# Three slots in lockstep at the RMS joints, constants multiplied while waiting, and a changed head and tail

## The reference

```python
def first_block(x, ...):
    for layer in range(2):
        x = x + 0.5 * rmsnorm(swiglu(rmsnorm(x, g[0]), gate0, up0, down0), g[1])
        x = x + rmsnorm(token_mixer(rmsnorm(x, g[2]), ...), g[3])
        x = x + 0.5 * rmsnorm(swiglu(rmsnorm(x, g[4]), gate1, up1, down1), g[5])

def second_block(x, ...):
    for l in range(2):
        proj = x @ w_in[l]
        mix = concatenate([hgrn2_mixer(...), nsa_mixer(...)]) @ w_out[l]
        x = layer_norm(ALPHA * x + mix, ...)
        x = layer_norm(ALPHA * x + swiglu(x, gate, up, down), ...)
```

## Time and profile before

| | us |
|---|---|
| median of 3 runs | 3538.73 (3535.65 to 3539.88) |
| the profiled execution, its own time | 3540.74 |
| its span, first to last instruction | 3538.9 |
| PE busy in it | 3402.1 (96%) |
| DVE, ACT, POOL busy | 1611.7, 1260.4, 1354.5 |

### The profile page before, as it was taken

How to read it: one execution, slowest core, us unless ns; L and a number is a source line. 1 busy time by engine, 2 the same in 40 slices (tenths; PEclk the granted TensorE clock), 3 DMA queues, 4 the chain that set the end, 5 groups by cost and what they waited for, 6 DMA issues and landing times. The chain is left out here.

```text
span 3538.9 us, 47749 instructions
## 1 busy us (share of the span) xinstructions
PE 3402.1 (96%) x17526; PEld 2702.6 (76%) x17526; DVE 1611.7 (46%) x2820; ACT 1260.4 (36%) x2129; POOL 1354.5 (38%) x582
## 2 busy tenths in 40 slices
PE   8999999999999999999999999989999999889998
PEld 6888866688878888766788878767888787568886
DVE  4441445554335432363644255774331358753322
ACT  3222346522232222265422244463222343642222
POOL 3444222244434444322344433304444443134443
PEclk9999999999999999999999999999999999999999
DMA  4222311222222222211222332202222321112222
GB/s 174 95 99 95 115 66 43 66 95 95 95 83 97 99 97 95 107 60 36 84 95 94 98 130 69 71 19 71 96 95 96 113 92 51 47 54 96 100 95 84
DMA packets 86780, 306.19 MB, mean 87 GB/s; under 512 B 11205, under 2 KB 11717, under 8 KB 85358
## 3 DMA queue, kind: packets, MB, share of 16 engines
q1 hardware_dynamic: 86400, 304.18, 25.6%
q10 hardware_dynamic: 238, 0.09, 0.0%
HBM read 299.49 MB, written 4.74 MB: 86 GB/s over the span
## 5 line engine op out<-in xcount | busy, mean ns | idle before, releaser
L338 POOL TENSOR_TENSOR wL<-ring,wH 128x1024 fp32r<-128x1024 f32 x513 | 1258.1, 2452 | 2112.3 <-ACT wH L328 2048.4
L288 PE MATMUL bank<-hH,wH 128*128 128x512 f32 x2448 | 966.0, 395 | 11.0 <-DVE yT L989 4.8
L328 ACT ACTIVATE wH<-ring 128x1024 fp32r<-128x1024 f32 x522 | 548.3, 1050 | 1157.5 <-PE bank L290 972.9
L290 PE MATMUL bank<-hH,wL 128*128 128x512 f32 x2448 | 954.5, 390 | 0.0
L289 PE MATMUL bank<-hL,wH 128*128 128x512 f32 x2448 | 953.7, 390 | 0.0
L288 PEld LDWEIGHTS bank<-hH,wH 128*128 128x128 f32 x2448 | 460.6, 188 | 111.6 <-issue 6.3
L290 PEld LDWEIGHTS bank<-hH,wL 128*128 128x128 f32 x2448 | 460.1, 188 | 96.9
L289 PEld LDWEIGHTS bank<-hL,wH 128*128 128x128 f32 x2448 | 460.6, 188 | 95.3 <-issue 1.9
L288 PE MATMUL bank<-guH,wH 128*128 128x512 f32 (+1 forms) x1292 | 502.9, 389 | 2.3 <-ACT early L1385 1.4
L290 PE MATMUL bank<-guH,wL 128*128 128x512 f32 (+1 forms) x1292 | 496.2, 384 | 0.0
L289 PE MATMUL bank<-guL,wH 128*128 128x512 f32 (+1 forms) x1100 | 418.6, 381 | 0.0
(11 more groups left out here) (347 smaller groups left out, 3863.9 us busy)
## 6 DMA issues: line engine op xcount, KB each, us to landing
ring<-in_w SPq DMA_DIRECT2D x376, 512.0 KB, 3.5
ring<-in_down SPq DMA_DIRECT2D x96, 448.0 KB, 3.2
ring<-in_down SPq DMA_DIRECT2D x48, 512.0 KB, 3.5
ring<-in_next SPq DMA_DIRECT2D x12, 512.0 KB, 3.4
mix<-in_table SPq DMA_DIRECT2D x2, 2560.0 KB
mix<-spread SPq DMA_DIRECT2D x4, 768.0 KB, 6.1
mix<-row SPq DMA_DIRECT2D x1, 2560.0 KB
spread<-mix SPq DMA_DIRECT2D x1, 2560.0 KB, 8.0
```

The source lines that it names most:

```text
L288: eng.matmul(out, a, hi, start=first, stop=False)
L290: return eng.matmul(out, b, hi, start=False, stop=last)
L328: eng.activation(parts_of(n, per)[0][:, 0:width], ring[:, n % NSLOT, 0:width], ACT.Copy).then_inc(w_hi, 1)
L338: eng.tensor_tensor(l[:, 0:width], ring[:, n % NSLOT, 0:width], h[:, 0:width], ALU.subtract).then_inc(w_lo, 1)
```

## The change

- The head makes three slots instead of two: slot 0 follows the pieces of hH and hL, slots 1 and 2 take their high part first and their low part last. ACT's gain load goes behind the three loads for the bias table; the squares go behind the third high part; DVE makes the low part of slot 1, POOL those of slots 2 and 3; SP loads five slots. The bias row is spread by one DMA from HBM to HBM.
- The four joints multiply three slots in lockstep (`joint_of`), the fourth slot's high part is made between chunks (`act_split`) and its low part by DVE after the last chunk. The third slot's high part stands ahead of the root, its low part ahead of DVE's first scaled chunk. Three more slots use dead tiles (`placed`).
- `keep_warm` multiplies the identity by constants into an unused PSUM bank: in `pe_stat_out` before and after the second statistics matmul. No result of it is read.
- Before the second FFN the squares go to PSUM banks 3 and 7, DVE adds them in another order, and ACT takes the high parts after columns 1, 3, 5 and 7.
- In block two, projection slot 2 is multiplied ahead of the layer's block, after the pair; five slots are loaded ahead instead of four.
- In the tail the mean is copied to SBUF, and POOL subtracts it from columns 4 to 7.

The diff, cut to what the prediction speaks of:

```diff
-        def pe_stat_out(eng, r):
+        def pe_stat_out(eng, r, before, after, into):
 
             eng.wait_ge(sq_used, 8 * r + 7 + 2)
             eng.matmul(bank[6][:, :], onesD, acc, start=True, stop=False, skip_group_check=True)
+            keep_warm(eng, before, into, S // 2)
             eng.wait_ge(sq_ready, 8 * r + 8)
             eng.matmul(bank[6][:, :], onesD, sq[:, 1, :], start=False, stop=True,
                        skip_group_check=True).then_inc(stat_ready, 1)
+            keep_warm(eng, after, into)
...
+        def act_split(eng, xr, gains, fourth):
...
+                if m == 4:
+                    hi(eng, fourth)
+                eng.wait_ge(x_ready, xr + m + 1)
+                eng.activation(hH[:, m, :], xT[:, m, :], ACT.Copy, scale=gains[:, m:m + 1]).then_inc(h_hi, 1)
+                eng.activation(yT[:, m, :], xT[:, m, :], ACT.Square).then_inc(xsq_ready, 1)
...
         def dve_post(eng, q, n, g, third, h0=None, gains=None, b=None):
...
+            vector_lo(eng, third)
             eng.wait_ge(rs_ready, q + 1)
-            vector_lo(eng, third)
+            vector_lo(eng, third + 1)
...
+        JOINT_BANKS = (0, 2, 1)
+
+        def joint_of(eng, n, h0, banks):
+
+            landed(eng, n + len(banks) - 1)
+            for kc in range(KD):
+                eng.wait_ge(h_hi, h0 + kc + 1)
+                for u, b in enumerate(banks):
+                    high, low = (v[:, kc * P:(kc + 1) * P] for v in parts_of(n + u))
+                    eng.matmul(bank[b][:, :], high, hH[:, kc, :], start=(kc == 0), stop=False, skip_group_check=True)
+                    eng.matmul(bank[b][:, :], low, hH[:, kc, :], start=False, stop=False, skip_group_check=True)
+                eng.wait_ge(h_ready, h0 + kc + 1)
+                for u, b in enumerate(banks):
+                    mm = eng.matmul(bank[b][:, :], parts_of(n + u)[0][:, kc * P:(kc + 1) * P], hL[:, kc, :],
+                                    start=False, stop=(kc == KD - 1), skip_group_check=True)
+                    if kc == KD - 1:
+                        mm.then_inc(slots_done, 1)
+
+        def keep_warm(eng, times, into, columns=S):
+
+            for _ in range(times):
+                eng.matmul(bank[into][:, 0:columns], ident, mats[:, 0:columns // P, :], start=True, stop=True,
+                           skip_group_check=True)
...
-            if n0:
-                eng.wait_ge(g_free, KF * c + 1)
+            eng.wait_ge(g_free, KF * c + 2)
+            if norm is not None:
                 pair_of(eng, n0, h0)
-            eng.wait_ge(g_free, KF * c + 2)
-            slot(0, 1, 0)
+                slot(0, 1, 0)
+            elif n0:
+                joint_of(eng, n0, h0, JOINT_BANKS)
             slot(0, 1, 1)
...
-                dve_y(eng, r, KD - 1)
+                eng.wait_ge(sq_ready, 8 * r + 8)
+                eng.tensor_copy(yT[:, KD - 1, :], bank[5][:, :]).then_inc(y_done, 1)
+                eng.wait_ge(stat_ready, 2 * r + 2)
+                eng.sem_inc(sq_used, 1)
...
-            if n0 and not third:
-                hi(eng, n0 + 2)
-            hi(eng, n0 + 3)
+            if stat is None:
+                hi(eng, n0 + 3)
...
             if not halves:
+                hi(eng, n0 + FFN_SLOTS + 2)
                 act_root(eng, q + 1, EPS_RMS)
...
+        OUT_SQ = (3, 7)
+
         def act_out1(eng):
 
             for m in range(KD):
                 eng.wait_ge(y_done, 8 + m + 3)
                 eng.wait_ge(sq_used, 8 + m + 1)
-                eng.activation(sq[:, m % 2, :], yT[:, m, :], ACT.Square).then_inc(sq_ready, 1)
-                if m in (1, 4, 6):
-                    hi(eng, n_out + A1 + 2 + (1, 4, 6).index(m))
+                to = bank[OUT_SQ[m % 2]][:, :] if m < KD - 1 else sq[:, 1, :]
+                eng.activation(to, yT[:, m, :], ACT.Square).then_inc(sq_ready, 1)
+                if m in (1, 3, 5, 7):
+                    hi(eng, n_out + A1 + 2 + (1, 3, 5, 7).index(m))
 
         def dve_out1(eng):
+
+            def add(m):
+                eng.wait_ge(sq_ready, 8 + m + 1)
+                if m == 0:
+                    eng.tensor_copy(acc, bank[OUT_SQ[0]][:, :]).then_inc(sq_used, 1)
+                    return
+                eng.wait_ge(sq_used, 8 + m + 2)
+                eng.tensor_tensor(acc, bank[OUT_SQ[m % 2]][:, :], acc, ALU.add).then_inc(sq_used, 1)
 
             eng.wait_ge(early_out, KD)
             for m in range(KD):
+                if m:
+                    add(m - 1)
                 eng.wait_ge(*tile_end(n_out + A1, B1, m, KD - 1))
                 eng.tensor_tensor(yT[:, m, :], bank[4 + m % 2][:, :], early[:, m, :], ALU.add).then_inc(y_done, 1)
-                if m:
-                    add_squares(eng, 1, m - 1)
-            add_squares(eng, 1, KD - 1)
+            eng.wait_ge(stat_ready, 4)
+            eng.sem_inc(sq_used, 1)
...
+            def high(n, kc, v, first=False):
+                return eng.matmul(bank[JOINT_BANKS[n]][:, :], parts_of(n)[0][:, kc * P:(kc + 1) * P], v[:, kc, :],
+                                  start=first, stop=False, skip_group_check=True)
+
+            def low(n, kc):
+                return eng.matmul(bank[JOINT_BANKS[n]][:, :], parts_of(n)[1][:, kc * P:(kc + 1) * P], hH[:, kc, :],
+                                  start=False, stop=(kc == KD - 1), skip_group_check=True)
+
+            eng.wait_ge(w_hi, 1)
+            for kc in range(KD + 1):
+                if kc < KD:
+                    eng.wait_ge(h_hi, kc + 1)
+                    high(0, kc, hH, kc == 0)
+                if kc:
+                    if kc == 1:
+                        landed(eng, 0)
+                    eng.wait_ge(h_ready, kc)
+                    high(0, kc - 1, hL)
+                    mm = low(0, kc - 1)
+            mm.then_inc(slots_done, 1)
+            for n in (1, 2):
+                eng.wait_ge(w_hi, n + 1)
+                for kc in range(KD):
+                    high(n, kc, hH, kc == 0)
+                    high(n, kc, hL)
                 landed(eng, n)
                 for kc in range(KD):
+                    mm = low(n, kc)
...
                 sp.dma_start(t["row"], rows8).then_inc(w_in1, 16)
-                for n in range(2, 4):
+                sp.dma_start(mats[:, :, :], t["mats"]).then_inc(par_in, 16)
+                for n in range(2, 5):
                     load(sp, n, t["first"][n, :, :], WIDE)
-                sp.dma_start(mats[:, :, :], t["mats"]).then_inc(par_in, 16)
                 sp.wait_ge(w_in1, 16)
 
-                sp.dma_start(spread, t["row"].unsqueeze(0).broadcast_to([P, NSA, 640])).then_inc(w_in1, 16)
-                sp.wait_ge(w_in1, 32)
-                sp.dma_start(t["spread"], spread).then_inc(bias_out, 16)
-                slot_sem(sp, 3)
+                sp.dma_start(t["spread"], t["row"].unsqueeze(0).broadcast_to([P, NSA, 640])).then_inc(bias_out, 16)
+                slot_sem(sp, 4)
...
-                act.dma_start(gnext, t["gfirst"]).then_inc(x_in[0], 16)
                 act.dma_start(onehot, t["onehot"]).then_inc(tab_in, 16)
                 act.dma_start(rb[0:32, :], t["rel_bias"]).then_inc(tab_in, 16)
                 act.dma_start(rb[32:33, :], t["one8"]).then_inc(tab_in, 16)
+                act.dma_start(gnext, t["gfirst"]).then_inc(x_in[0], 16)
                 act.preload_act_table_set(EXP_LN)
                 hi(act, 0)
-                act_split(act, None, gnext, True, early_slot=1)
+                for m in range(KD):
+                    if m == 2:
+                        hi(act, 1)
+                    act.wait_ge(x_in[m // 2], 16 if m // 2 else 32)
+                    act.activation(hH[:, m, :], xT[:, m, :], ACT.Copy, scale=gnext[:, m:m + 1]).then_inc(h_hi, 1)
                 hi(act, 2)
+                for m in range(KD):
+                    act.activation(yT[:, m, :], xT[:, m, :], ACT.Square).then_inc(xsq_ready, 1)
+                hi(act, 3)
 
             @block.vector
             def _(dve):
                 for n, c in enumerate((0, 320)):
                     dve.wait_ge(c_out, n + 1)
                     dve.tensor_copy(rows8[:, c:c + 320], bank[4 + n][0:8, 0:320]).then_inc(c_done, 1)
-                vector_lo(dve, 0)
+                dve.wait_ge(w_hi, 1)
+                dve.tensor_tensor(parts_of(0)[1], ring[:, 0, :], parts_of(0)[0], ALU.subtract).then_inc(w_lo, 1)
                 for m in range(KD):
                     rest(dve, 0, m, gnext)
+                vector_lo(dve, 1)
...
             def _(pool):
-                los(pool, 1, 3)
+                los(pool, 2, 4)
...
+                       n_ffn1: (place(guH, 16), place(guH, 18), n_out + A1),
+                       n_next: (place(guH, 0), place(guH, 2), n_next - 2),
+                       n_next + 2: (place(guH, 4), place(guH, 6), n_next - 2)})
...
-                    stream(sp, layer, t["next_1"], 0, 4, n_next, WIDE)
-                    slot_sem(sp, n_next + 3)
```

(50 more changed lines are left out.)

76 lines of the change are left out of this document (25 added, 51 removed).

## The result

The changed kernel takes 3522.3 us (median; 3518.2 to 3525.2 in 4 runs) against 3537.9 for the kernel before on the same chip: a ratio of 0.9949, 95% interval 0.9937 to 0.9961. The forecast was 3522.6. The profiled span is 3523.2 us against 3538.9.

What follows compares the result with a forecast made beforehand. PE, busy 96% of the span, was taken as the bound; only its idle, half clock, head and tail could save time. 7.6 + 10.2 + 2.3 - 1.6 - 4.6 + 2.2 = 16.1 off 3538.73 gave 3522.6 us, range 3512 to 3533.

Steps and rivals of the forecast that it cites:

- Head: Start of the kernel to the first layer block: slot 3 starts at 30.5 instead of 39.21; 7.6 us gained (4 to 10).
- rival D: Head: loads and tables queue behind the HBM to HBM bias spread, slower from 32 us of transfer on; chance 0.05.
- Joints before the FFN: Two RMS joints before block one's second FFNs: slot 3 begins at 690.2 instead of 695.26; 5.1 us each, 10.2 in both.
- Ln comes about 1.5 earlier: Joints before the FFN: with squares in PSUM, DVE's adds take 0.7, so Ln comes 1.5 us earlier (0.5 to 1.8).
- priced half clock at half its length: RMS joints: half-clock stretches of 6.9 us before and 3.4 us behind the FFN cost half their length and go.
- Joint after the FFN: Block one, layer 0: slot 3 starts at 1063.1 instead of 1066.55, less 1.1 for the sums; 2.3 us gained (1 to 5).
- Into block two: Joint into the second block: a new 3.2 us wait ahead of slot 6, plus half clock; -1.6 us (-4 to +3.2).
- Layer 0 to 1: Second block, between its layers: the block opens 5.5 us later; 2.9 lost and 1.7 for the clock, -4.6 us (-7 to 0).
- Tail: Last layer norm: four subtractions of about 0.6 us leave DVE's chain for POOL; 2.2 us gained (-3.4 to 2.4).
- A: Second block: no new wait, as slot 6's split gets through early; 9.6 us more gained, 3513 us; chance 0.13.
- B: RMS joints: the constants don't hold the clock; 6 x 1.7 = 10.2 us less gained, 3532.8 us; chance 0.17.
- C: Four joints: ACT's early split meets a slot not landed, Ln waits up to 1.7 us each; 3529.4 us; chance 0.10.

Runs made afterwards that it cites:

- control 2: The changed kernel run again, not altered, on the same chip as the runs beside it: 3523.3 us, 0.9948 of the kernel before.

## Why the prediction was right, point by point

- **Head**: right, 7.9 for 7.6. Slot 3 came at 30.0 to 31.1, by the mean where it was worked out, and the collision at the sums cost 0.57 instead of 1.1: the split met the second sum, as expected, and the sums ended 6.4 us after their start, but PE asked later, at 36.8 - 31.1 = 5.7. This account is read from the timelines; no run puts the head back alone. The spread, rival D, took 12.8 us and nobody waited for it.
- **Joints before the FFN**: the sum is right, its parts are not. The step "Ln comes about 1.5 earlier" gave 0.8 behind the last output tile (3.0 us, where it was 3.8) and some 0.3 more ahead of it, though the squares in PSUM are worth 3.4 to 3.6 by themselves in the new order: the reason given (adds of 0.7) was right, and the rest of the change took most of it back, by what is open but for the half-width constant. The step that priced half clock at half its length was wrong at these joints: with a pair 6.9 us of it cost some 0.3, in lockstep 3.4 us cost 1.05, and only in the FFN did 3.4 us cost 1.6. So the lockstep carries these joints (without it 3.3 us are lost, all of the 3.2 gained there), and the constants (0.90 us each, worked out as 0.92) add 1.0 to it, as they keep PE, which now sets the pace, at full clock. The prediction's account of the pace itself, 2.07 us of PE a chunk over 1.92 of DVE, was the right step: 66 matmuls stood behind the first hL, and they ran without waits.
- **Joint after the FFN**: right, 2.5 for 2.3; without constants 1.9 of it would go. Lockstep wasn't tested alone here.
- **Into block two**: the wait of 3.2 was there (3.07, released by POOL's split, 19.67 us after the opening where 19.8 were worked out). Behind it the same program ran at half clock for 6.9, 0 or 3.4 us, and the stage lost 2.6, won 0.3 or lost 1.6. The forecast of -1.6 lies among these, and its one stretch of 3.4 us is one case of three.
- **Layer 0 to 1**: right to 0.1, wait and clock both (2.72 to 3.07 us of wait, then 3.4 us at half clock in all three profiles), and put back by moving the slot alone.
- **Tail**: POOL's part was 2.25 for 2.2; 0.8 more came with the last store's landing.
- **Not foreseen**: 0.9 won in the first FFNs and 2.5 lost in block two, layer 1, most of it clock stretches that come and go between executions of one program. Together they lose 1.6, and the tail, the head and the two kinds of joint had won 1.5 more than forecast, so the total of 3522.6 owes part of its closeness to luck; the terms themselves were off by up to 2.5.
- **Rivals**: A fell, as the order on ACT decided. B fell, since the clock held; its price, 10.2 us, was also too high, 4.0 at the joints by the run without constants. C fell before the FFN: the early split ended at 660.3, ahead of Ln at 660.56, which waited 0.30 us, for PE. Behind the FFN it showed once, far below its price of 1.7: in control 2 the split ahead of block two waited 0.50 us for its load, and PE stood 0.51 us ahead of hH. D fell.

## What to carry to other kernels

Before half clock is priced, ask who sets the pace in that stretch: 3.4 us cost 1.6 where PE did, and 6.8 us cost 0.3 to 1.2 where PE waited for another engine's pieces. More work per piece (three slots for two) makes PE the one that sets the pace, and there keeping the clock up with constant matmuls pays more (1.0 us for each 3.4, against 1.2 for 6.8 at the layer norms). A stage that is met just in time takes back what an earlier arrival gains, with half clock on top; move work behind its opening, not ahead of it.

## What the runs showed of the hardware

- One program shows half-clock stretches at different places in different executions: 61, 72 and 75 us of them in sum ahead of the tail in its three profiles; the times of one program spread by 3 to 8 us.
- The compression's matmuls of 62 columns took 7.33 us at full clock, or 11.3 (2101.59 - 2090.28) with half clock over most of them, with 0.73 us of idle 2.6 us ahead of the stretch.
- In the last layer norm DVE's subtraction and scaling, each with one input in PSUM, took 0.68 and 0.74 us beside POOL's subtractions in SBUF, no more than without them; an add with both inputs in SBUF took 1.9 instead of 0.69 beside a split of POOL, and ended 0.55 us after it.
